# Up projection of a hybrid block: whole PSUM banks are copied by token, and DMAs move the blocks to their features' partitions

## The chip, the cores and the metric

The kernel runs on one core of one Trainium2 chip. The metric is the device time of one execution in microseconds (us). The kernel before takes 1037.89 us, the median of three runs (1037.18 to 1038.49).

## The reference

One layer of a hybrid encoder block in float32, for 256 tokens of width 2048: an input projection, two kinds of attention, an output projection `w_o` with a residual, and then the gated feed-forward part that this case is about:

```python
def conv_gated_ffn(h, w_up, conv_w, conv_b, w_down):
    S = h.shape[1]
    u = h @ w_up
    up = jnp.pad(u, ((0, 0), (CONV_W - 1, 0), (0, 0)))
    c = conv_b + sum(up[:, j:j + S] * conv_w[j] for j in range(CONV_W))
    gate, val = c[..., :D_FF], c[..., D_FF:]
    return (jax.nn.silu(gate) * val) @ w_down
...
        h = rms_norm(x, norm_ffn[l])
        x = x + conv_gated_ffn(h, w_up[l], conv_w[l], conv_b[l], w_down[l])
```

`w_up` is 2048 x 11264 (D_FF is 5632), `w_down` 5632 x 2048. `rms_norm` divides each token by its root mean square and multiplies each feature by a gain. The convolution (width 3) runs over tokens, with taps of each feature's own.

## The kernel before

**Products.** Each float32 operand is split in two: ScalarE copies a weight tile to a rounded type (`hi`, line 641), VectorE subtracts it from the tile (`lo`, line 1000). TensorE makes three products of each pair (hi x hi and lo x hi in `hi2`, lines 1523 and 1524; hi x lo in `lo1`, line 1528). A tile of weights is 512 KB. The stages follow each other: projection in, attention, `w_o`, up projection, down projection, final norm.

**The ring.** Raw tiles lie in a ring of four. SyncE (SP) issues the load of tile t when VectorE has made the `lo` part of tile t - 4 (`load`, lines 427 to 430). ScalarE and VectorE split three tiles ahead of TensorE (`LEAD`): while TensorE works on tile s, they make tile s + 3. ScalarE's split also waits until TensorE is done with tile t - 4, whose split buffer it takes.

**The up stage.** It has 22 steps: 11 pairs `j`, each with `v` = 0 (gate) and `v` = 1 (value). A step is 8 tiles, and gives 256 tokens x 512 features, tokens on partitions, in two PSUM banks: `tr_ps` for `v` = 0, `pj` for `v` = 1. The convolution wants features on partitions. So while TensorE works on the next step, the step just ended is finished by the other engines (its `s` counts the 8 tiles of that next step):

- `s` = 0 to 3: ScalarE copies the 16 blocks of 32 partitions each to other partitions, into `moved` (`move_blocks`, line 857), in groups of 5, 4, 4 and 3. The banks are free for TensorE after the last.
- `s` = 4: VectorE transposes `moved` in 32 x 32 squares into `ub` (line 1257) and multiplies by the tokens' roots, spread over all partitions in `r2b` (`scale_rows`, line 1264). That comes ahead of the `lo` split of tile 7.
- `s` = 5, 6: ScalarE starts the convolution (line 866). `s` = 6, 7: VectorE ends it (lines 1270 and 1274).
- With `v` = 1 also the gate: VectorE's product at `s` = 0 (line 1281), ScalarE's rounded copy (line 878) and VectorE's remainder (line 1286) at `s` = 1.

The order on each engine is the order in which the code is written; semaphores do the rest. TensorE waits for the blocks of two steps ago before it writes a bank again. SP's queue holds only the loads there, and POOL's queue builds sums of `w_down` tiles in DRAM all through the stage. The last step is finished in the first tiles of the down stage, with half of its blocks moved by VectorE (line 1414).

**The roots.** After `w_o`, the tokens' roots are made by VectorE and ScalarE, turned, written to DRAM by four small DMAs (line 844) and read back for all partitions (line 847).

**Other DMAs from SBUF to SBUF.** Attention (line 437) and `w_o` (line 491) already turn blocks with a DMA: four DMAs for each time, each from 32 partitions to all 128.

Of the kernel before, what the change touches and what calls it, by code (L numbers as in the profile page):

```python
# [5 lines left out]
F32 = mybir.dt.float32  # L6
# [5 lines left out]
P = 128  # L12
# [24 lines left out]
UP_DVE_STEPS = 10  # L37
# [88 lines left out]
MOVES = {0: (0, 5), 1: (5, 9), 2: (9, 13), 3: (13, SIDE * SIDE)}  # L126
# [69 lines left out]
def program(nc, x, norm_mix, w_in, sinks, b_f, w_o, norm_ffn, w_up, conv_w, conv_b, w_down, norm_final,  # L196
            ident_c, tri_c, mask_b_c, cos_c, sin_c, out):
    ctx = ExitStack()
    with ctx:
# [6 lines left out]
        def sem(name):  # L206
# [14 lines left out]
        r2b = sb("r2b", [P, S])  # L221
# [7 lines left out]
        region_end = sbuf.cursor  # L229
        sbuf.cursor = region  # L230
# [40 lines left out]
        moved = sb("moved", [P, 4, MT, SIDE, BLOCK])  # L271
# [69 lines left out]
        y_s, yturn_s, yhi_s, ylo_s, ysq_s, y2_tot, y2_root, r2_s, r2_out, d_r2 = (sem(n) for n in (  # L341
            "y_s", "yturn_s", "yhi_s", "ylo_s", "ysq_s", "y2_tot", "y2_root", "r2_s", "r2_out", "d_r2"))
        d_y = [sem(f"d_y{i}") for i in range(2)]
        pad_s, moved_s, moved_d, u_s, c0_s, conv_s, silu_s, gated_s, ghi_s, glo_s = (sem(n) for n in (
            "pad_s", "moved_s", "moved_d", "u_s", "c0_s", "conv_s", "silu_s", "gated_s", "ghi_s", "glo_s"))
# [9 lines left out]
        r2_dram = nc.dram_tensor("r2_dram", (MT, SIDE, BLOCK), F32).ap()  # L355
# [51 lines left out]
        r2_block, r2_rows = conv_o[:, 1, 0, 0:BLOCK], conv_o[:, 0, 0, 0:BLOCK]  # L407
        r2c = r2_block[:, 0:MT]
# [11 lines left out]
        def _(sp):  # L420
# [87 lines left out]
            with sp.Fori(1, UP_PAIRS) as j:  # L508
# [120 lines left out]
        def _(act):  # L629
# [191 lines left out]
            def y_hi_turned(n):  # L821

                act.wait_ge(d_y[n % 2], (n // 2 + 1) * PARTS_Y)
                for b in range(4):
                    k = 4 * n + b
                    act.activation(act_hi[:, k].rearrange("p (a x) -> p a x", a=SIDE), y_turned[n % 2][:, b], ACT.Copy, scale=g2[:, k:k + 1]).then_inc(yhi_s, 1)
# [9 lines left out]
            def root_of_squares(s):  # L836
# [4 lines left out]
                if s == 3:  # L841
                    act.wait_ge(r2_s, 3)
                    for a in range(SIDE):
                        act.dma_start(r2_dram[:, a], r2_rows[a * BLOCK:a * BLOCK + MT]).then_inc(r2_out, 16)
                if s == 5:
                    act.wait_ge(r2_out, 16 * SIDE)
                    act.dma_start(r2b[:], r2_dram.rearrange("m a i -> (m a i)").partition_broadcast(P)).then_inc(d_r2, 16)
# [12 lines left out]
            def conv_first(j, v, pair):  # L860

                act.wait_ge(u_s, step_of(j, v, 2, pair + 1))
# [18 lines left out]
            def finish(j, v, s):  # L881

                if s in MOVES:
                    ins = move_blocks(j, v, *MOVES[s], step_of(j, v, UP_TILES, T_UP + UP_TILES))
                    if MOVES[s][1] == SIDE * SIDE:
                        ins.then_inc(moved_s, 1)
# [51 lines left out]
            half = SIDE * SIDE // 2  # L938
            for t in range(DOWN_END):
                if t == 6:  # L940
# [4 lines left out]
                if t < 2:  # L945
                    ins = move_blocks(*last_step, t * half // 2, (t + 1) * half // 2, T_DOWN)
                if t == 1:
                    ins.then_inc(moved_s, 1)
                if t == 1:
                    silu_gate(UP_PAIRS - 1)  # L950
                if t in (3, 4):
                    conv_first(*last_step, t - 3)
                if t == 7:
# [34 lines left out]
        def _(dve):  # L988
# [230 lines left out]
            def y_lo_turned(n):  # L1219

                for b in range(4):
                    k = 4 * n + b
                    dve.wait_ge(yhi_s, k + 1)
                    dve.scalar_tensor_tensor(act_lo[:, k].rearrange("p (a x) -> p a x", a=SIDE),
                                             y_turned[n % 2][:, b], g2[:, k:k + 1],
                                             act_hi[:, k].rearrange("p (a x) -> p a x", a=SIDE).bitcast(F32),
                                             ALU.mult, ALU.subtract).then_inc(ylo_s, 1)
# [11 lines left out]
            def root_of_squares(s):  # L1239

                if s == 0:
                    dve.memset(r2_block, 0.0).then_inc(r2_s, 1)
                    dve.wait_ge(ysq_s, MT * GROUPS)
                    dve.tensor_reduce(tot2, ss2, AX.X, ALU.add).then_inc(y2_tot, 1)
                if s == 2:
                    dve.wait_ge(y2_root, 1)
                    dve.wait_ge(r2_s, 1)
                    dve.reciprocal(r2c, root2).then_inc(r2_s, 1)
                    dve.wait_ge(r2_s, 2)
                    dve.transpose(r2_rows, r2_block).then_inc(r2_s, 1)  # L1250

            def turn_moved(j, v):

                dve.wait_ge(moved_s, step_of(j, v, 1, 1))
# [669 lines left out]
```

## Time and profile before

| | |
|---|---|
| median of 3 runs | 1037.89 us (1037.18 to 1038.49) |
| span of the profiled execution | 1035.4 us |
| median less span | 2.5 us |
| TensorE busy | 1026.6 us (99%) |
| VectorE busy | 793.9 us (77%) |
| ScalarE busy | 734.5 us (71%) |
| granted TensorE clock, mean | 0.999 |

The span is that of one profiled execution, from its first to its last instruction. No time of its own is given for that execution; the 2.5 us by which the median is above the span is taken for what lies around the span. Busy shares are means over stages. The up stage runs from about 323 us to about 801 us of the span.

### The profile page before, as it was taken

How to read it: one execution, taken by the hardware profiler on the slowest of the kernel's cores; microseconds unless marked ns; L12 is line 12 of the kernel's file. 1: busy time of each engine (PE TensorE's matmuls, PEld its weight loads, DVE VectorE, ACT ScalarE, POOL GpSimd, SP SyncE). 2: the span in 40 equal slices, each digit the busy share in tenths (PEclk: the TensorE clock that was granted, in tenths of full speed). 3: DMA queues.
4: the chain of work that ended last, by engine and by line, in shares of the span. 5: the costliest groups of instructions: out<-in, count | busy, mean ns of one | idle time of the engine just before them, and what ended most of it. 6: DMA issues, size and time to landing. Idle time of an engine off the chain costs nothing.

```text
span 1035.4 us, 15993 instructions
## 1 busy us (share of the span) xinstructions
PE 1026.6 (99%) x5141; PEld 858.3 (83%) x5141; DVE 793.9 (77%) x1026; ACT 734.5 (71%) x1191; POOL 88.9 (9%) x150
## 2 busy tenths in 40 slices
PE   9999999999999999999999999999999999999997
PEld 8888888888888888888888888888888878888885
DVE  5679787887767578768687787876868999887677
ACT  6966474745556687988879888798887766646664
POOL 1000000000111111111111111111111000000000
PEclk9999999999999999999999999999999999999999
DMA  9676767667899999898999998989999589888993
GB/s 295 188 225 178 238 189 224 191 208 215 271 285 321 282 290 269 264 266 278 264 288 254 280 263 269 282 254 278 261 274 264 167 306 316 295 289 285 319 313 113
DMA packets 156103, 266.85 MB, mean 258 GB/s; under 512 B 11908, under 2 KB 60388, under 8 KB 155936
## 3 DMA queue, kind: packets, MB, share of 16 engines
q1 hardware_dynamic: 138224, 222.67, 65.7%
q0 software_dynamic: 17360, 43.22, 18.9%
q8 instruction: 22, 0.36, 0.1%
q10 hardware_dynamic: 480, 0.47, 0.1%
q14 instruction: 17, 0.14, 0.0%
HBM read 256.86 MB, written 44.06 MB: 291 GB/s over the span
## 4 chain that ended last, share of the span: by engine, by line
PE 98%; DMA 1%; SPq 0%; DVE 0%; ACT 0%; issue 0%; DVEq 0%
PE pj L1523 12%; PE pj L1528 12%; PE pj L1524 12%; PE pj L1536 9%; PE tr_ps L1528 9%; PE tr_ps L1523 9%; PE tr_ps L1524 9%; PE pj L1541 5%; PE sc_ps L1528 4%; PE sc_ps L1523 4%; PE sc_ps L1524 4%; PE pj L1558 3%; PE pj L1551 2%; PE pj L1517 1%; PE pj L1519 1%; PE pj L1518 1%
## 5 line engine op out<-in xcount | busy, mean ns | idle before, releaser
L1000 DVE TENSOR_TENSOR split<-raw,split 128x1024 fp32r<-128x1024 f32 x265 | 321.6, 1222 | 159.6 <-ACT split L641 153.8
L641 ACT ACTIVATE split<-raw 128x1024 fp32r<-128x1024 f32 x259 | 272.7, 1056 | 125.1 <-PE pj L1528 26.0
L929 ACT ACTIVATE split<-raw 128x1024 fp32r<-128x1024 f32 (+1 forms) x125 | 121.6, 989 | 63.6 <-PE sc_ps L1528 27.9
L1335 DVE TENSOR_TENSOR split<-raw,split 128x1024 fp32r<-128x1024 f32 (+1 forms) x125 | 138.2, 1136 | 31.0 <-ACT split L929 29.3
L1523 PE MATMUL tr_ps<-split,act_split 128*128 128x512 f32 x352 | 136.9, 389 | 0.0
L1524 PE MATMUL tr_ps<-split,act_split 128*128 128x512 f32 x352 | 136.9, 389 | 0.0
L1523 PE MATMUL pj<-split,act_split 128*128 128x512 f32 x352 | 136.9, 389 | 0.0
L1524 PE MATMUL pj<-split,act_split 128*128 128x512 f32 x352 | 136.9, 389 | 0.0
L1536 PE MATMUL pj<-act_split,split 128*128 128x512 f32 x416 | 131.6, 398 | 0.0
L1528 PE MATMUL tr_ps<-split,act_split 128*128 128x512 f32 x352 | 94.1, 389 | 0.0
L1528 PE MATMUL pj<-split,act_split 128*128 128x512 f32 x352 | 94.1, 389 | 0.0
L1541 PEld LDWEIGHTS pj<-act_split,split 128*128 128x128 f32 x416 | 78.1, 188 | 18.4
L1541 PE MATMUL pj<-act_split,split 128*128 128x256 f32 x416 | 81.8, 278 | 0.0
L1524 PEld LDWEIGHTS pj<-split,act_split 128*128 128x128 f32 x352 | 66.1, 188 | 13.8
L1524 PEld LDWEIGHTS tr_ps<-split,act_split 128*128 128x128 f32 x352 | 66.1, 188 | 13.8
L1528 PEld LDWEIGHTS tr_ps<-split,act_split 128*128 128x128 f32 x352 | 66.1, 188 | 13.7
L1528 PEld LDWEIGHTS pj<-split,act_split 128*128 128x128 f32 x352 | 66.1, 188 | 13.7
L1523 PEld LDWEIGHTS tr_ps<-split,act_split 128*128 128x128 f32 x352 | 66.0, 188 | 13.7
L1523 PEld LDWEIGHTS pj<-split,act_split 128*128 128x128 f32 x352 | 66.0, 188 | 13.7
L857 ACT ACTIVATE moved<-tr_ps 32x256 f32<-32x256 f32 x176 | 66.3, 377 | 2.6
L857 ACT ACTIVATE moved<-pj 32x256 f32<-32x256 f32 x168 | 63.3, 377 | 2.5
L1536 PEld LDWEIGHTS pj<-act_split,split 128*128 128x128 f32 x416 | 63.3, 189 | 1.3 <-issue 1.3
(249 smaller groups left out, 1660.9 us busy)
## 6 DMA issues: line engine op xcount, KB each, us to landing
raw<-w_up SPq DMA_DIRECT2D x176, 512.0 KB, 5.8
raw<-w_in SPq DMA_DIRECT2D x72, 512.0 KB, 4.3
raw<-w_down SPq DMA_DIRECT2D x68, 512.0 KB, 6.0
t_dram<-w_down POOLq DMA_DIRECT2D x60, 512.0 KB, 6.6
raw<-t_dram SPq DMA_DIRECT2D x40, 512.0 KB, 6.0
raw<-w_o SPq DMA_DIRECT2D x32, 512.0 KB, 6.3
t_dram<-t_dram POOLq DMA_DIRECT2D x40, 256.0 KB, 6.6
raw<-w_down SPq DMA_DIRECT2D x20, 256.0 KB, 6.1
```

Source lines behind the costliest of these rows:

```text
L641: ins = act.activation(hi[:, slot, 0:TILE], raw[:, slot, 0:TILE], ACT.Copy)
L857: ins = act.activation(moved[b * BLOCK:(b + 1) * BLOCK, :, a % 2, a // 2::2].rearrange("p w m i -> p m w i"), rows, ACT.Copy)
L929: act.activation(hi[:, slot, c0:TILE], down_raw(t)[:, c0:TILE], ACT.Copy).then_inc(hi_done, 1)
L1000: dve.tensor_tensor(lo[:, slot, 0:n], raw[:, slot, 0:n], hi[:, slot, 0:n].bitcast(F32), ALU.subtract).then_inc(lo_done, 1)
L1335: dve.tensor_tensor(lo[:, slot, c0:TILE], down_raw(t)[:, c0:TILE], hi[:, slot, c0:TILE].bitcast(F32), ALU.subtract).then_inc(lo_done, 1)
L1523: pe.matmul(dst, a_hi, b_hi, start=start, stop=False, skip_group_check=True)
L1524: pe.matmul(dst, a_lo, b_hi, start=False, stop=False, skip_group_check=True)
L1528: return pe.matmul(dst, a_hi, b_lo, start=False, stop=True, skip_group_check=True)
L1536: pe.matmul(pj[:, 2 * pair + b], wh[:, c, b * P:(b + 1) * P], act_both(4 * kt + c), start=first and c == 0, stop=False, skip_group_check=True)
L1541: ins = pe.matmul(pj[:, 2 * pair + b, 0:S], wl[:, c, b * P:(b + 1) * P], act_hi[:, 4 * kt + c], start=False, stop=True, skip_group_check=True)
L1551: pe.matmul(pj[:, 2 + m, 0:S], act_lo[:, 4 * kt + c, m * P:(m + 1) * P], both[:, c, 0], start=first and c == 0, stop=False, skip_group_che ...
L1558: ins = pe.matmul(pj[:, 2 + m], act_hi[:, 4 * kt + c, m * P:(m + 1) * P], both[:, c].rearrange("p a n -> p (a n)"), start=False, stop=True ...
```

## The change

ScalarE copies each of the two banks of a step whole, scaled by the root of the partition's token, into a new tile `token_u`. SP then issues 16 DMAs of 32 KB each from `token_u` to `moved` (`move_u`), which stand in its queue ahead of the load of the third tile of a step (`MOVE_AT`). VectorE waits for all 16, and transposes in two instructions; the product with the roots goes, and so do the roots' way over DRAM, and VectorE's part in moving the last step. TensorE now waits for the evacuation alone. In the down stage the convolution of the last step comes two tiles later. A small rearrangement keeps the tokens of `act_hi` and `act_lo` in another order, for which VectorE's instruction on each block is cut in two.

```diff
-UP_DVE_STEPS = 10
+UP_DVE_STEPS = 8
...
-MOVES = {0: (0, 5), 1: (5, 9), 2: (9, 13), 3: (13, SIDE * SIDE)}
+PARTS_U = 16 * SIDE * SIDE
+MOVE_AT = 2
+LAST_MOVE_AT = 8
...
+            def move_u(j, v):
+
+                sp.wait_ge(evac_u, step_of(j, v, 1, 1))
+                for a in range(SIDE):
+                    for b in range(SIDE):
+                        sp.dma_start(moved[b * BLOCK:(b + 1) * BLOCK, a], token_u[a * BLOCK:(a + 1) * BLOCK, b]).then_inc(d_mv, 16)
+
             def up_loads(j, first):
                 for v in range(2):
                     for kt in range(UP_TILES):
+                        if not first and kt == MOVE_AT:
+                            move_u(j - 1, v)
                         load(step_of(j, v, UP_TILES, T_UP + kt), kt % RING, wide(raw, kt % RING),
...
             for t, (g, kind, part, kt) in enumerate(DOWN):
+                if t in (MOVE_AT, LAST_MOVE_AT):
+                    move_u(UP_PAIRS - 1, (MOVE_AT, LAST_MOVE_AT).index(t))
...
-            def move_blocks(j, v, first, last, tiles_done):
-
-                act.wait_ge(mm_done, tiles_done)
-                if not (isinstance(j, int) and 2 * j + v == 0):
+            def evacuate_u(j, v):
+
+                act.wait_ge(mm_done, step_of(j, v, UP_TILES, T_UP + UP_TILES))
+                if isinstance(j, int) and 2 * j + v == 0:
+                    act.wait_ge(r2_s, 1)
+                else:
                     act.wait_ge(u_s, step_of(j, v, 2, 0))
-                for i in range(first, last):
-                    a, b = divmod(i, SIDE)
-                    rows = up_banks[v][a * BLOCK:(a + 1) * BLOCK].rearrange("p m (w b i) -> p m w b i", w=4, b=SIDE)[:, :, :, b]
-                    ins = act.activation(moved[b * BLOCK:(b + 1) * BLOCK, :, a % 2, a // 2::2].rearrange("p w m i -> p m w i"), rows, ACT.Copy)
-                return ins
+                for m in range(MT):
+                    ins = act.activation(token_u[:, :, m].rearrange("p b w i -> p w b i"),
+                                         up_banks[v][:, m].rearrange("p (w b i) -> p w b i", w=4, b=SIDE), ACT.Copy, scale=r2c[:, m:m + 1])
+                ins.then_inc(evac_u, 1)
...
             def turn_moved(j, v):
 
-                dve.wait_ge(moved_s, step_of(j, v, 1, 1))
+                dve.wait_ge(d_mv, step_of(j, v, PARTS_U, PARTS_U))
                 if not (isinstance(j, int) and 2 * j + v == 0):
                     dve.wait_ge(conv_s, step_of(j, v, 4, 0))
-                st.done(dve.transpose(ub[:, :, 2:S + 2], moved[:].rearrange("p w m a i -> p w (m a i)")))
-
-            def scale_rows():
-
-                st.wait()
-                for pair in range(2):
-                    rows = ub[:, 2 * pair:2 * pair + 2, 2:S + 2]
-                    dve.tensor_tensor(rows, rows, r2b[:].unsqueeze(1).broadcast_to([P, 2, S]), ALU.mult).then_inc(u_s, 1)
+                for m in range(MT):
+                    dve.transpose(ub[:, :, m * P + 2:(m + 1) * P + 2].rearrange("p w (a x) -> p w a x", a=SIDE),
+                                  moved[:, :, m].rearrange("p a w i -> p w a i")).then_inc(u_s, 1)
...
-                    pe.wait_ge(moved_s, step_of(j, v, 1, -1))
+                    pe.wait_ge(evac_u, step_of(j, v, 1, -1))
```

SP's queue in the loop over the pairs, before the change: the loads of a step follow each other, each behind its wait for `lo_done` (the `lo` part of four tiles before).

```order
L430 ISA [waits lo_done]
L430 DMA raw<-w_up 128x2x512
L429 REGISTER_ALU
L430 ISA [waits lo_done]
L430 DMA raw<-w_up 128x2x512
```

The same place after the change, where the loads of a step's second and third tile stood next to each other:

```order
L431 ISA [waits lo_done]
L431 DMA raw<-w_up 128x2x512
L498 REGISTER_ALU
L501 DMA moved<-token_u 32x256 [waits evac_u]
L501 DMA moved<-token_u 32x256 x15
L430 REGISTER_ALU
L431 ISA [waits lo_done]
L431 DMA raw<-w_up 128x2x512
```

Sixteen DMAs now stand between two loads, once in each step.

VectorE at `s` = 4 and 5 of a step with `v` = 0, before the change (`split<-raw` is the `lo` part of tile 7, then of tile 8):

```order
L1256 ISA [waits moved_s]
L1257 STREAM_TRANSPOSE ub<-moved 128x4x256 [waits conv_s]
L177 ISA
L1264 TENSOR_TENSOR ub<-ub,r2b 128x2x256 [waits dve_step]
L1264 TENSOR_TENSOR ub<-ub,r2b 128x2x256
L993 REGISTER_ALU
L1000 TENSOR_TENSOR split<-raw,split 128x1024 [waits hi_done]
```

And after it:

```order
L1259 ISA [waits d_mv]
L1261 STREAM_TRANSPOSE ub<-moved 128x4x128 [waits conv_s]
L1261 STREAM_TRANSPOSE ub<-moved 128x4x128
L997 REGISTER_ALU
L1004 TENSOR_TENSOR split<-raw,split 128x1024 [waits hi_done]
```

The wait ahead of the transposes was one for ScalarE and is now one for the DMAs; the `lo` part of tile 7 stands behind it as before.

## Rows read from the trace of the kernel before

**Rows 1.** The page's first part: busy time, share of the span, instructions.

```profile
PE 1026.6 (99%) x5141; PEld 858.3 (83%) x5141; DVE 793.9 (77%) x1026; ACT 734.5 (71%) x1191; POOL 88.9 (9%) x150
```

**Rows 2.** Windows: busy us by engine (instructions), TensorE clock, DMA share, GB/s.

```profile
320.00:324.00 4.00, 4.00 (x19) 3.30 (x19) 1.54 (x2) 2.04 (x2) 0.52 (x1) 1.00 1.01 365
...
411.00:454.50 43.50, 43.50 (x194) 36.02 (x193) 32.42 (x39) 36.53 (x61) 6.09 (x10) 1.00 0.90 264
454.50:498.00 43.50, 43.50 (x194) 36.02 (x193) 33.88 (x43) 36.64 (x61) 5.84 (x10) 1.00 0.91 277
```

**Rows 3.** Waits of TensorE's weight loads on VectorE: us in total, times, longest.

```profile
PEld pj L1517 <- DVE act_split L1016: 0.8, 1, 0.8
...
PEld sc_ps L1528 <- DVE split L1335: 0.4, 1, 0.4
...
PEld tr_ps L1528 <- DVE split L1335: 0.3, 1, 0.3
```

**Rows 4.** Groups of instructions: busy us, mean ns of one, idle before.

```profile
L857 ACT ACTIVATE moved<-tr_ps 32x256 f32<-32x256 f32 x176 | 66.3, 377 | 2.6
...
L1264 DVE TENSOR_TENSOR ub<-ub,r2b 128x512 f32<-128x512 f32 x44 | 28.5, 688 | 0.8
L1257 DVE STREAM_TRANSPOSE ub<-moved 128x1024 f32<-128x1024 f32 x22 | 27.4, 1246 | 1.2
...
L1216 DVE STREAM_TRANSPOSE prob_t<-nat 128x512 f32<-128x512 f32 x8 | 8.4, 1094 | 0.1
...
L755 ACT ACTIVATE mix_hi<-tr_ps 128x512 f32 x6 | 3.6, 595 | 1.0 <-PE tr_ps L1659 1.0
```

**Rows 5.** Timeline of VectorE around one step: start us, us, instruction.

```profile
454.59 0.88 DVE L1270 SCALAR_TENSOR_TENSOR conv_o<-ub,cst,conv_o 128x256 f32<-128x256 f32 x2
...
456.41 1.23 DVE L1000 TENSOR_TENSOR split<-raw,split 128x1024 fp32r<-128x1024 f32 x1
...
461.81 1.22 DVE L1000 TENSOR_TENSOR split<-raw,split 128x1024 fp32r<-128x1024 f32 x1 [1.28 <-ACT split L641]
...
468.12 1.22 DVE L1000 TENSOR_TENSOR split<-raw,split 128x1024 fp32r<-128x1024 f32 x1
...
477.98 1.23 DVE L1281 TENSOR_TENSOR conv_o<-conv_o 128x1024 f32<-128x1024 f32 x1
479.12 2.36 DVE L1000 TENSOR_TENSOR split<-raw,split 128x1024 fp32r<-128x1024 f32 x2
```

**Rows 6.** Timeline of TensorE: first product of that step, last four of its tile 7.

```profile
453.78 0.39 PE L1523 MATMUL tr_ps<-split,act_split 128*128 128x512 f32 x1
...
474.63 1.07 PE L1528 MATMUL tr_ps<-split,act_split 128*128 128x512 f32 x4
```

**Rows 7.** Timeline of SP: the load issued behind the `lo` part of tile 5.

```profile
463.20 0.37 SPq L430 DMA_DIRECT2D raw<-w_up  x1
```

**Rows 8.** Line 430, loads of `w_up`: ns to issue (min/median/max), us to landing.

```profile
L430 SPq DMA_DIRECT2D raw<-w_up x176: 362/373/592, 310.6 to 785.1; - x176
...
DMA to landing us min/median/max: 3.4/5.5/11.4
```

**Rows 9.** Line 491, SBUF to SBUF, 32 partitions to 128: ns to issue, us to landing.

```profile
L491 SPq DMA_DIRECT2D prob<-prob_t x16: 548/604/654, 275.2 to 330.2; - x16
...
DMA to landing us min/median/max: 2.8/3.2/8.0
```

**Rows 10.** Line 537, results from 128 partitions, behind each other: issue, landing.

```profile
L537 SPq DMA_DIRECT2D result<-nat x9: 333/442/453, 1025.7 to 1031.6; - x9
...
DMA to landing us min/median/max: 1.9/2.4/3.4
```

**Rows 11.** Line 844, ScalarE's queue, 2 partitions each: ns to issue.

```profile
L844 ACTq DMA_DIRECT2D r_dram<-conv_o x4: 242/275/482, 331.7 to 332.7; - x4
```

**Rows 12.** Line 437, SBUF to SBUF in the attention stage: ns to issue.

```profile
L437 SPq DMA_DIRECT2D prob<-prob_t x48: 542/603/1054, 91.0 to 249.7; - x48
```

More of the change, by code:

```diff
@@ L229, in program @@
         region_end = sbuf.cursor
+        sbuf.cursor = region_end - 4 * 4 * S
+        token_u = sb("token_u", [P, SIDE, MT, 4, BLOCK])
         sbuf.cursor = region
@@ L406, in program @@
         root2 = small[:, 38:40]
-        r2_block, r2_rows = conv_o[:, 1, 0, 0:BLOCK], conv_o[:, 0, 0, 0:BLOCK]
-        r2c = r2_block[:, 0:MT]
+        r2c = small[:, 40:42]
         g1 = cst[:, 0:KB]
@@ L507, in _ @@
             up_loads(0, True)
-            with sp.Fori(1, UP_PAIRS) as j:
+            up_loads(1, False)
+            with sp.Fori(2, UP_PAIRS) as j:
                 up_loads(j, False)
             for t, (g, kind, part, kt) in enumerate(DOWN):
+                if t in (MOVE_AT, LAST_MOVE_AT):
+                    move_u(UP_PAIRS - 1, (MOVE_AT, LAST_MOVE_AT).index(t))
                 if t < RING:
@@ L881, in finish @@
             def finish(j, v, s):
[L883 to L886, printed above, removed]
+                if s == 0:
+                    evacuate_u(j, v)
                 if s in (5, 6):
@@ L937, in _ @@
             last_step = (UP_PAIRS - 1, 1)
-            half = SIDE * SIDE // 2
             for t in range(DOWN_END):
-                if t == 6:
+                if t == 8:
                     act.activation(small[:, 24:25], eps, ACT.Sqrt)
@@ L944, in _ @@
                     down_hi(t + LEAD)
[L945 to L948, printed above, removed]
+                if t == 0:
+                    evacuate_u(*last_step)
                 if t == 1:
                     silu_gate(UP_PAIRS - 1)
-                if t in (3, 4):
-                    conv_first(*last_step, t - 3)
-                if t == 7:
+                if t in (5, 6):
+                    conv_first(*last_step, t - 5)
+                if t == 9:
                     gated_hi(UP_PAIRS - 1)
@@ L1246, in root_of_squares @@
                     dve.wait_ge(y2_root, 1)
-                    dve.wait_ge(r2_s, 1)
                     dve.reciprocal(r2c, root2).then_inc(r2_s, 1)
-                    dve.wait_ge(r2_s, 2)
-                    dve.transpose(r2_rows, r2_block).then_inc(r2_s, 1)
             def turn_moved(j, v):
-                dve.wait_ge(moved_s, step_of(j, v, 1, 1))
+                dve.wait_ge(d_mv, step_of(j, v, PARTS_U, PARTS_U))
                 if not (isinstance(j, int) and 2 * j + v == 0):
                     dve.wait_ge(conv_s, step_of(j, v, 4, 0))
-                st.done(dve.transpose(ub[:, :, 2:S + 2], moved[:].rearrange("p w m a i -> p w (m a i)")))
-            def scale_rows():
-                st.wait()
-                for pair in range(2):
-                    rows = ub[:, 2 * pair:2 * pair + 2, 2:S + 2]
-                    dve.tensor_tensor(rows, rows, r2b[:].unsqueeze(1).broadcast_to([P, 2, S]), ALU.mult).then_inc(u_s, 1)
+                for m in range(MT):
+                    dve.transpose(ub[:, :, m * P + 2:(m + 1) * P + 2].rearrange("p w (a x) -> p w a x", a=SIDE),
+                                  moved[:, :, m].rearrange("p a w i -> p w a i")).then_inc(u_s, 1)
             def conv_rest(j, v, pair):
@@ L1304, in up_step @@
                             turn_moved(p, b)
-                            if first:
-                                dve.wait_ge(d_r2, 16)
-                            scale_rows()
                         if s == 0 and v == 1 and not first:
@@ L1407, in gain @@
                                          gfin[:, n * 512:(n + 1) * 512], ALU.mult)
-            def move_blocks(first, last):
-                for i in range(first, last):
-                    a, b = divmod(i, SIDE)
-                    rows = up_banks[1][a * BLOCK:(a + 1) * BLOCK].rearrange("p m (w b i) -> p m w b i", w=4, b=SIDE)[:, :, :, b]
-                    dve.tensor_copy(moved[b * BLOCK:(b + 1) * BLOCK, :, a % 2, a // 2::2].rearrange("p w m i -> p m w i"), rows).then_inc(moved_d, 1)
-            half = SIDE * SIDE // 2
-            dve.wait_ge(mm_done, T_DOWN)
             for t in range(DOWN_END):
-                if t == 2:
-                    dve.wait_ge(moved_d, half)
-                if t == 2:
+                if t == 4:
                     turn_moved(UP_PAIRS - 1, 1)
@@ L1428, in _ @@
                     down_lo(t + LEAD)
-                if t < 2:
-                    move_blocks(half + t * half // 2, half + (t + 1) * half // 2)
-                if t == 2:
-                    scale_rows()
-                if t in (4, 5):
-                    conv_rest(UP_PAIRS - 1, 1, t - 4)
-                if t == 6:
+                if t in (6, 7):
+                    conv_rest(UP_PAIRS - 1, 1, t - 6)
+                if t == 8:
                     gate(UP_PAIRS - 1)
-                if t == 7:
+                if t == 9:
                     gated_lo(UP_PAIRS - 1)
```

41 lines of the change are left out of this document (18 added, 23 removed).

## The prediction

> **What bounds the kernel now.** I read the page's first part, then windows of two whole steps each in the up stage, then the waits of TensorE, then the timelines of VectorE, TensorE and SP through one step. The page has TensorE busy for 1026.6 us of 1035.4 [rows 1], and in the windows it is busy for all of 43.50 us, with the full clock, while VectorE has 9.6 to 11.1 us free and ScalarE 6.9 [rows 2]. The waits on VectorE add up to 1.5 us, and none is in the up stage [rows 3]. So TensorE's own work is the bound: two steps are 43.5 us, a step 21.75, a tile 2.72. Work taken off ScalarE or VectorE there buys nothing; the question is what the new chain of waits costs.
>
> **What goes.** ScalarE: 16 copies of 0.377 us in a step, 6.0 us, become 2 of about 0.60 (a copy of 128x512 from PSUM, 595 ns) [rows 4], 1.2 us. VectorE: two products of 0.688 go. The transpose of 1.246 us becomes two of half the width: between 0.62 each (half of it) and 1.09 (line 1216, as wide, but it picks every fourth element) [rows 4]. I take 0.62, because the new one reads whole runs of 32 as the old one does; the other end would cost 0.95 us more in a step. All of this is hidden under TensorE. The end of the block moves by VectorE, the roots' way over DRAM, and the cut of VectorE's 16 instructions at the `w_o` stage come to a few us on engines that TensorE doesn't wait for there: 0, bounds -1.5 (all of the waits in [rows 3]) and +1. In the down stage the convolution starts two tiles later, with five tiles left until its result is wanted: 0.
>
> **What comes: a chain round SP, the DMAs and VectorE.** In SP's queue the 16 DMAs stand behind the load that waits for the `lo` part of tile 5. They must all land before VectorE transposes, and behind the transpose stands the `lo` part of tile 7, which TensorE wants at 474.63, that is 20.85 us after the step's start at 453.78 [rows 6]. How long are they?
>
> - Start. VectorE made the `lo` part of tile 5 from 461.81, and the load went out at 463.20 [rows 5, 7], 9.4 us after the start. ScalarE's block copies hold that back now; without them the rounded copy of tile 5 starts when TensorE starts tile 2, at 5.45, and ends at about 6.5, the `lo` part at 7.8, and the load's issue (0.37, [rows 8]) at 8.3.
> - Issue. No DMA of before goes from 32 partitions to 32. The nearest rows: 0.604 us for one from 32 partitions to 128, SBUF to SBUF [rows 9], and 0.603 for others of that kind [rows 12]; 0.442 for results behind each other from 128 partitions [rows 10]; 0.373 for a load [rows 8]; 0.275 for one of two partitions [rows 11]. With a gap of 0.03 from one to the next the pitch is between 0.30 and 0.64. The new DMA moves 32 plain rows on both sides, which puts it between the one of 2 rows and those of 128, and it has no change of shape between its sides, which the 0.604 has. I take 0.40. Fifteen pitches are 6.0 us (4.5 to 9.6).
> - Landing of the last, from the start of its issue: 2.4 median in rows 10, 3.2 in rows 9 of which 0.6 is issue. I take 2.6 (2.3 to 3.2).
>
> First step: 8.3 + 6.0 + 2.6 = 16.9, transposes 1.25, `lo` part 1.22 (the length in [rows 5]): 19.4. TensorE wants it at 20.85, so it has 1.45 us to spare.
>
> But the chain closes on itself. The next 16 DMAs wait for the `lo` part of the next step's tile 5, and VectorE works in order: from one pair of transposes to that point it has 7 `lo` parts. Two successive steps, added up:
>
> - VectorE: 4 transposes 2.5; 14 `lo` parts at 1.2 (2.36 for two behind each other, 1.22 alone, [rows 5]) 16.8; 16 convolution instructions, four of which take 454.59 to 456.41, 1.85 with their gaps [rows 5], 7.4; gate product and its remainder at 1.15 each (477.98 to 479.12, [rows 5]) 2.3. Sum 29.0.
> - SP and DMAs, twice: 0.1 for the hand-over, 0.4 for the load, 6.0, 2.6: 9.1 each, 18.2.
>
> Together 47.2 us against TensorE's 43.5: 3.7 in two steps, 1.85 in one. That VectorE is free for a quarter of the time [rows 2] doesn't help, as it sits in front of the wait. ScalarE isn't in the chain: the load of the third tile goes out 6.4 us after the DMAs' start, lands 5.5 later [rows 8], at 11.9, and VectorE wants its `lo` part at about 15.5.
>
> There are 21 turns of a step inside the up stage, 20 distances between them. TensorE is late at the end by 20 x 1.85 - 1.45 = 35.5 us, and can't win it back, since it has no idle time to give. Span 1035.4 + 35.5 = 1070.9; with the 2.5 us by which the median of the runs is above the span, 1073.4.
>
> The Trainium skill speaks against this size. Its page "DMA: Bandwidth & Descriptors", in the section on the anatomy of one DMA, puts most of a DMA's fixed 2 us down to the wait for the write's receipt and calls the making of descriptors small; "SBUF — State Buffer", on the set-up-cost knee, gives sequencer and descriptor work as some 50 ns and a few hundred. With 0.25 us as an estimate from that page the chain would fit and the change would cost nothing, which is the first rival below. The trace has no SBUF-to-SBUF issue under 0.54 [rows 9, 12]; it sides against the low end.
>
> **The rivals.**
>
> 1. *The chain fits, and the time stays.* It decides at one number: 2 x (0.5 + 15 x pitch + landing) + 29.0 = 43.5, so pitch x 15 + landing = 6.75, a pitch of 0.29 with a landing of 2.4. For it: an issue of 0.275 on a small DMA [rows 11]. Against: the other rows are all above 0.33. VectorE wouldn't hold TensorE up, and the time would be 1038. Chance 0.15.
> 2. *The issue costs what rows 9 and 12 have.* Pitch 0.64: 15 x 0.64 + 2.6 = 12.2, two steps 29.0 + 25.4 = 54.4, 5.45 too much in each; the first turn is late by 2.15 at once. 20 x 5.45 + 2.15 = 111, time 1149. For it: the same kind of memory on both sides, the same 32 source partitions, runs of 1 KB. Against: there 128 rows stand on the target side. Chance 0.17.
> 3. *The DMA engines become the bound.* A step moves about 270 GB/s x 21.75 us = 5.9 MB at a share of 0.905 [rows 2]; full share at that mix is 298 GB/s. 0.52 MB more makes 6.4 MB, 21.5 us: it just fits. If the moves take twice their share it is 23.2, and 20 steps cost 29 us: 1067. Against: a stretch of 4 us ran at 365 GB/s [rows 2]. Chance 0.08.
> 4. *Faster.* The engines that feed TensorE have more room, and the waits of rows 3 and the tail shrink: 1.5 us at most, 1036.4. A gain past 0.2% would need more than all of them. Chance 0.03.
>
> **How the numbers follow.** The forecast, the chain with a pitch of 0.33 to 0.50, has 0.57; its own range is 1045 (pitch 0.33 with a landing of 2.4: 15.7 + 29.0 = 44.7, 0.6 in a step) to 1110 (pitch 0.50 with 2.8: 3.45 in a step, and 0.25 late at the first turn, 69; 1107). The range for 8 in 10 takes in the upper bound of the issue, 1149, and at the low end reaches just over rival 1, whose time is the floor of the likely ones: 1038 to 1150. Within 0.2% is 1035.8 to 1040.0, about what a measurement of this kernel can tell from no change. Faster 0.03; the same 0.15; slower 0.57 + 0.17 + 0.08 = 0.82.
>
> **What would show it.** In the profile after: TensorE has idle time in the up stage, in front of the third product (line 1528 of before), released by VectorE's `lo` part, once in each step at tile 7, and about 3.7 us in two steps. VectorE's largest new wait is that of the transposes for the DMAs from `token_u`. SP issues the 16 in about 6.4 us. ScalarE is busy for about 27 us of two steps where it had 36.6. The down stage keeps its length. I am wrong if TensorE stays at its 43.5 us for two steps (the issue is cheap), if it waits for rounded copies that wait for raw tiles (the loads are the bound, rival 3), or if the waits stand in the down stage.

## The result, and the profile after

The changed kernel takes 1169.61 us (median of 4 runs, 1165.20 to 1171.50) against 1037.72 for the kernel before: a ratio of 1.126 (95% interval 1.124 to 1.129), 131.9 us slower. Ratios here and below are of fast executions alone; one slow execution of the kernel before, of 3689 us beside the first experiments, is not in them. The forecast was 1073 with a range up to 1150. The sign and the place were right, the size was not: the loss is 3.7 times the one forecast, and above rival 2's too.

The page of the kernel after, busy time by engine and the granted clock in 40 slices:

```profile
PE 1064.5 (91%) x5141; PEld 878.6 (75%) x5141; DVE 760.1 (65%) x1010; ACT 634.0 (54%) x891; POOL 89.9 (8%) x150
...
PEclk9999999999999989898988989999989999999999
...
PE 47%; SPq 18%; DVE 15%; DMA 10%; issue 7%; ACT 2%; DVEq 1%; ACTq 0%
```

Against [rows 1] VectorE has lost 34 us of work and ScalarE 100, as the change meant, and the span has grown from 1035.4 to 1165.9. The third line, the shares of the chain that ended last, has 18% of SP issuing and 10% of DMAs landing. TensorE's busy time has risen by 38 us with the same 5141 products; the clock line shows where: the slices below full clock are all in the up stage. The run `fill` below prices that.

Window of the kernel after, the stretch of [rows 2] in one piece (busy us by engine, clock, DMA share, GB/s):

```profile
411.00:498.00 87.00, 72.85 (x299) 58.93 (x298) 44.10 (x56) 43.60 (x51) 9.55 (x16) 0.92 0.82 226
```

TensorE was busy for all 87 us and is now for 72.85, with 299 products recorded where there were 388. The share of the DMA engines was 0.90 to 0.91 and is 0.82: they are not what is short. The waits say what is:

```profile
DVE ub L1261 <- DMA moved<-token_u: 239.7, 22, 13.3
ACT conv_o L875 <- DVE ub L1261: 168.1, 21, 11.6
...
ACT split L654 <- DMA raw<-w_up: 75.1, 50, 5.0
...
PE pj L1510 <- DVE split L1004: 55.0, 11, 8.3
...
PE tr_ps L1510 <- DVE split L1004: 33.4, 10, 5.4
```

VectorE waits 22 times for the moves, 10.9 us each on average; TensorE waits 21 times for VectorE's `lo` part, once in a step. (In [rows 3] the waits on VectorE were under 1 us each.) The timeline of SP shows the reason in its length: 10.0 us for 16 moves, with the loads queued behind them.

```profile
500.88 13.36 SPq L431 DMA_DIRECT2D raw<-w_up  x7
514.40 10.03 SPq L501 DMA_DIRECT2D moved<-token_u  x16
524.68 17.54 SPq L431 DMA_DIRECT2D raw<-w_up  x8
542.32 10.09 SPq L501 DMA_DIRECT2D moved<-token_u  x16
552.77 0.38 SPq L431 DMA_DIRECT2D raw<-w_up  x1
```

The chain of waits in 515 to 569 us (start, us, what) is the closed ring, piece by piece: moves, their landing, VectorE's transposes, its `lo` parts, a load, and the next moves. It has no TensorE in it; between its lines below stand more of the moves and VectorE's `lo` parts and convolution instructions:

```profile
514.97 0.59 SPq L501
515.60 0.59 SPq L501
...
523.20 0.59 SPq L501
523.84 4.80 DMA moved<-token_u
...
529.30 0.67 DVE ub L1261
529.97 2.24 DVE split L1004 x2
...
539.27 2.42 DVE split L1004 x2
541.84 0.37 SPq L431
542.32 0.51 SPq L501
...
551.20 0.58 SPq L501
551.82 2.17 DMA moved<-token_u
```

From 514.97 to 515.60 is the pitch: 0.63 us. Over most of the up stage (345 to 920 us) the chain isn't as pure: issues of moves are 32.5% of it and their landing 10.4%, but raw tiles' landing is 5.0% and TensorE's products at least 9.3%. All moves of the kernel (ns to issue, min/median/max; us to landing):

```profile
L501 SPq DMA_DIRECT2D moved<-token_u x352: 512/591/1175, 353.4 to 941.3; - x176
...
DMA to landing us min/median/max: 1.8/3.5/7.2
```

**Where the 130.5 us of span went.** TensorE's first product of the up stage starts at 323.12 (323.22 before), its first of the down stage at 924.24 (801.94 before): 122.4 us in the up stage. Another 8.2 us are in the down stage (233.5 us before, 241.7 after). There the last step's moves still hold VectorE up, and TensorE then waits for it 1.0 us at 947.6 and 2.6 us at 960.5; the clock is below its full value in parts of the stage (0.85 in 924 to 934 us, 0.86 in 954 to 964). The two waits are 3.5 us, and TensorE is busy for 230.5 us of the stage where it was for 226.6: 7.4 of the 8.2 us. With four DMAs in place of 16 on the same queue (`four`), or with nobody waiting for four (`cut4`), the down stage has 233.4 and 233.5 us. VectorE's timeline there, and TensorE's wait at the first turn (window 323 to 370):

```profile
943.24 1.30 DVE L1261 STREAM_TRANSPOSE ub<-moved 128x512 f32<-128x512 f32 x2 [6.64 <-DMA moved<-token_u]
...
PE pj L1510 <- DVE split L1004: 1.3, 1, 1.3
```

In the up stage the 20 distances between the transposes (364.74 to 920.46 us) average 27.79 us where a step was 21.75: 20 x 6.04 = 120.8. The rest, 1.6, is mostly the first turn, where TensorE waited for the 1.3 us in the line above.

Worked out over those 20 distances from the timelines of SP and VectorE, with the same for three kernels of the experiments:

| mean, us | turn to first move | SP issuing | end of issue to turn | step | 20 x (step - 21.75) | measured loss |
|---|---|---|---|---|---|---|
| forecast | 15.0 | 6.4 | 2.2 | 23.6 | 37 | |
| after, 16 moves | 15.19 | 10.12 | 2.48 | 27.79 | 121 | 131.9 |
| `eight` | 15.29 | 5.23 | 4.80 | 25.32 | 71 | 71.6 |
| `four` | 15.47 | 2.64 | 6.08 | 24.19 | 49 | 50.1 |
| `r4sp` | 15.16 | 2.82 | 7.40 | 25.38 | 73 | 77.7 |

The last two columns agree because the loss lies in the up stage, evenly over its steps; of what `r4sp` and the kernel after lose beyond that, most is in the down stage. What makes a step long is in the three columns before.

### The profile page after: what moved, and what is told of

The parts are those of the page before. It is cut to its first block, busy times and chain, and to the rows that moved or that the text cites. A ratio compares the mean times of both kernels' runs of the same rounds, so it can differ in the third digit from the quotient of the medians.

```text
span 1165.9 us, 15889 instructions
## 1 busy us (share of the span) xinstructions
PE 1064.5 (91%) x5141; PEld 878.6 (75%) x5141; DVE 760.1 (65%) x1010; ACT 634.0 (54%) x891; POOL 89.9 (8%) x150
## 4 chain that ended last, share of the span: by engine, by line
PE 47%; SPq 18%; DVE 15%; DMA 10%; issue 7%; ACT 2%; DVEq 1%; ACTq 0%
SPq L501 17%; DVE split L1004 9%; PE pj L1518 8%; DMA moved<-token_u 5%; PE pj L1510 5%; PE pj L1523 4%; DMA raw<-w_up 4%; PE pj L1505 4%; PE pj L1506 4%; PE sc_ps L1510 3%; PE sc_ps L1505 3%; PE sc_ps L1506 3%; PE pj L1540 3%; PE tr_ps L1505 2%; PE tr_ps L1506 2%
## 5 line engine op out<-in xcount | busy, mean ns | idle before, releaser
L1004 DVE TENSOR_TENSOR split<-raw,split 128x1024 fp32r<-128x1024 f32 x265 | 317.9, 1217 | 93.5 <-ACT split L654 87.3
L654 ACT ACTIVATE split<-raw 128x1024 fp32r<-128x1024 f32 x259 | 273.0, 1058 | 193.2 <-DMA raw<-w_up 75.1
L1261 DVE STREAM_TRANSPOSE ub<-moved 128x512 f32<-128x512 f32 x44 | 28.7, 690 | 239.7 <-DMA moved<-token_u 239.7
L1510 PE MATMUL pj<-split,act_split 128*128 128x512 f32 x352 | 102.5, 416 | 55.0 <-DVE split L1004 55.0
L1505 PE MATMUL tr_ps<-split,act_split 128*128 128x512 f32 x352 | 143.6, 408 | 0.0
L1506 PE MATMUL tr_ps<-split,act_split 128*128 128x512 f32 x352 | 142.5, 405 | 0.0
L1505 PE MATMUL pj<-split,act_split 128*128 128x512 f32 x352 | 141.3, 402 | 0.0
L1506 PE MATMUL pj<-split,act_split 128*128 128x512 f32 x352 | 141.2, 401 | 0.0
L875 ACT ACTIVATE conv_o<-ub,cst 128x256 f32<-128x256 f32 x88 | 47.8, 590 | 168.1 <-DVE ub L1261 168.1
L1510 PE MATMUL tr_ps<-split,act_split 128*128 128x512 f32 x352 | 99.0, 404 | 33.4 <-DVE split L1004 33.4
L1510 PEld LDWEIGHTS pj<-split,act_split 128*128 128x128 f32 x352 | 69.5, 201 | 74.0 <-DVE split L1004 59.7
L1510 PEld LDWEIGHTS tr_ps<-split,act_split 128*128 128x128 f32 x352 | 67.4, 194 | 51.5 <-DVE split L1004 37.7
L1505 PEld LDWEIGHTS tr_ps<-split,act_split 128*128 128x128 f32 x352 | 70.2, 199 | 15.4
L1506 PEld LDWEIGHTS tr_ps<-split,act_split 128*128 128x128 f32 x352 | 70.1, 199 | 15.4
L1505 PEld LDWEIGHTS pj<-split,act_split 128*128 128x128 f32 x352 | 68.9, 196 | 14.9
L1506 PEld LDWEIGHTS pj<-split,act_split 128*128 128x128 f32 x352 | 68.7, 195 | 14.9
```

The costliest lines, as they stand in the source:

```text
L654: ins = act.activation(hi[:, slot, 0:TILE], raw[:, slot, 0:TILE], ACT.Copy)
L875: act.activation(conv_o[:, v, w], ub[:, w, 2:S + 2], ACT.Identity, scale=tap(2, j * 4 + (w + v * FB)), bias=tap(3, j * 4 + (w + v * FB))). ...
L1004: dve.tensor_tensor(lo[:, slot, 0:n], raw[:, slot, 0:n], hi[:, slot, 0:n].bitcast(F32), ALU.subtract).then_inc(lo_done, 1)
L1505: pe.matmul(dst, a_hi, b_hi, start=start, stop=False, skip_group_check=True)
L1506: pe.matmul(dst, a_lo, b_hi, start=False, stop=False, skip_group_check=True)
L1510: return pe.matmul(dst, a_hi, b_lo, start=False, stop=True, skip_group_check=True)
```

## The experiments

Each time is a median; beside it stands the kernel before, run on the same chip (1037.4 to 1038.6 us).

**micro: what an issue costs, by itself.** A small program, executed once, in which SP issues DMAs in groups of 8 or 4 with nothing else running. (At its end ScalarE issues eight while SP writes the results; these had a median of 0.765 us, outside of what theory A expected, and with SP busy beside them they don't tell what ScalarE's queue costs by itself.)

```
sp.dma_start(cross[b*32:(b+1)*32, a], src[a*32:(a+1)*32, b])   # 32 rows of 1 KB; short: 128 B; pair: 16 rows
sp.dma_start(full[:, ...], src[:, ...])                        # 128 rows of 512 B; fan: 32 partitions to 128
sp.dma_start(d32[...], src[...])                               # to DRAM; down, wide: from DRAM
sp.dma_start(alone[...], src[...]); wait                       # one at a time
```

> This kernel computes nothing of the block: it only issues small DMAs of several forms in groups, and writes zeros. It measures the issue by itself. Theory A (the issue of a DMA from SBUF to SBUF costs about 0.59 us whatever its size, because of the kind): 32 rows of 1 KB, 32 rows of 128 B, 16 rows and 128 rows from SBUF to SBUF all take 0.55 to 0.65 us to issue, on SP as on ScalarE's queue, and those with DRAM on one side 0.33 to 0.45. Theory B (the cost comes from the rows or from a full queue of descriptors): 16 rows or 128 B rows issue in under 0.45 us, the 128 rows take over 0.8, and a DMA that is issued alone takes under 0.45.

```profile
L51 SPq DMA_DIRECT2D cross<-src x8: 565/590/596, 3.0 to 7.5; - x8
L57 SPq DMA_DIRECT2D short<-src x8: 507/591/592, 9.3 to 13.6; - x8
L62 SPq DMA_DIRECT2D full<-src x8: 528/601/602, 15.3 to 19.8; - x8
L67 SPq DMA_DIRECT2D fan<-src x4: 605/611/629, 21.7 to 23.7; - x4
L73 SPq DMA_DIRECT2D d<-src x8: 362/422/423, 26.3 to 29.5; - x8
L79 SPq DMA_DIRECT2D down<-w_down x8: 355/421/423, 31.1 to 34.3; - x8
L84 SPq DMA_DIRECT2D wide<-w_down x4: 349/432/432, 36.0 to 37.3; - x4
L90 SPq DMA_DIRECT2D pair<-src x8: 581/589/591, 39.9 to 44.3; - x8
L96 SPq DMA_DIRECT2D alone<-src x8: 507/507/507, 46.1 to 58.5; - x8
```

The medians fall into two values: 0.59 to 0.61 us where both sides are SBUF, 0.42 to 0.43 where one is DRAM (`d` and `down` have the 32 rows of 1 KB of `cross`). Rows (16, 32, 128) and row length (128 B to 1 KB) change it by 0.02 at most. Issued singly it is 0.507, the value of the first one in a step of the kernel. Landing with the engines idle has medians of 1.7 to 1.9 us from SBUF to SBUF, 2.6 for `fan`.

**four: a quarter of the DMAs, the same bytes, the wait kept.** The 32x32 blocks are not exchanged, so what VectorE turns is not the reference's.

```
                 for a in range(SIDE):
-                    for b in range(SIDE):
-                        sp.dma_start(moved[b * BLOCK:(b + 1) * BLOCK, a], token_u[a * BLOCK:(a + 1) * BLOCK, b]).then_inc(d_mv, 16)
+                    sp.dma_start(moved[:, a], token_u[:, a]).then_inc(d_mv, 16)
```

> The changed kernel with the 512 KB of a step moved by 4 DMAs of 128 rows of 1 KB, partition to same partition, in place of 16 of 32 rows: same bytes, same waits, blocks not moved to their features' partitions. Theory A (a closed chain of SP's issues, the landing, and VectorE's order): a step of 27.8 us loses 12 issues of 0.63, 7.6 us, and is 20.2, under TensorE's 21.75; time 1038 to 1043, TensorE's waits in the up stage under 3 us in all. Theory B (the bytes on the DMA engines are the bound): nothing or little changes, 1150 or more. Theory C (each DMA costs by its rows): 128 rows take four times the issue, and the time stays at 1150 or more as well, but with SP's issues at 2.4 us.

1088.73 us, ratio 1.050 (1.045 to 1.054): 81 us less than the kernel after, but 50 above before, where none was expected. The issue did shrink to 2.64 us; the landing grew.

```profile
L500 SPq DMA_DIRECT2D moved<-token_u x88: 470/601/2176, 353.2 to 858.0; - x88
...
DMA to landing us min/median/max: 3.4/5.9/10.4
```

5.9 us to land, not 1.9 as in `full` (of half the size). In the kernel after a long issue hid this. Worked out from the trace, the first of its 16 moves lands 5.2 us after the start of its issue on average and the last 3.0, where the four of `four` have 5.8 to 6.7. `short` below, with an eighth of the bytes, has the same 5.0 falling to 2.9, so it isn't the moves' own bytes. The likely reason is that no load is added while SP issues the 16, and the last finds the engines free; that is argued, not shown. Issue time taken away comes back in part as landing: of 7.48 us less, 3.60.

**cut: the 16 DMAs stay, VectorE doesn't wait for them.** VectorE turns `token_u` itself, unexchanged. ScalarE's next copies wait for the moves, since these read `token_u`; no such wait shows in the trace.

```
-                dve.wait_ge(d_mv, step_of(j, v, PARTS_U, PARTS_U))
+                dve.wait_ge(evac_u, step_of(j, v, 1, 1))
```

> The changed kernel, but VectorE transposes token_u itself, as soon as ScalarE has written it; the 16 DMAs are issued in the same place and nobody but ScalarE's next evacuation (and the first use of their memory in the down stage) waits for them. Blocks aren't moved. It keeps SP's blocked queue, the late loads and the traffic, and takes the wait away. Theory A (chain through VectorE's wait): 1038 to 1045; SP's 10.1 us of issues in a step of 21.75 fit beside 8 loads of 0.4. Theory B (SP's queue holds back the loads of raw tiles, and TensorE starves for them): TensorE still waits, for rounded copies that wait for raw tiles, and the time is above 1080.

1113.15 us, ratio 1.072 (1.068 to 1.076). The wait is gone and 75 us of loss are there all the same. The two views of `cut`, waits and SP's timeline:

```profile
ACT split L654 <- DMA raw<-w_up: 222.5, 93, 9.6
...
577.47 10.03 SPq L501 DMA_DIRECT2D moved<-token_u  x16
587.86 14.27 SPq L431 DMA_DIRECT2D raw<-w_up  x8
602.28 3.06 SPq L501 DMA_DIRECT2D moved<-token_u  x5
```

From moves to moves it is 24.8 us: 10.0 in which no load goes out, and 14.3 in which all eight of a step have to (the row takes in SP's waits for free tiles). The held queue makes the loads late, and ScalarE waits for raw tiles. The prediction had taken the loads to be safe (the load of the third tile "goes out 6.4 us after the DMAs' start" and lands "at 11.9, and VectorE wants its `lo` part at about 15.5"); with 10 us of issue they are not.

**early: the moves at the step's start** (`MOVE_AT` 2 becomes 0), everything computed.

> The changed kernel with the 16 DMAs two loads earlier in SP's queue (MOVE_AT 0). Theory A: between the transposes and the next DMAs VectorE has 5 lo parts in place of 7, 2.4 us less in a step, and the remainder of the gate product (1.15 in two steps) falls behind them: a step is 27.8 - 2.4 - 0.6 = 24.8, time 1169.6 - 20 x 3.0 = 1110 (1100 to 1120). Theory B (DMA engines or SP as a whole are the bound): no change, 1165 to 1172.

1151.15 us (1146.25 and 1156.05), ratio 1.108 (1.102 to 1.115): 18 us less than the kernel after, not the 50 to 70 expected. Its waits:

```profile
ACT split L654 <- DMA raw<-w_up: 255.3, 77, 11.6
DVE ub L1261 <- DMA moved<-token_u: 182.1, 22, 11.1
```

The wait for raw tiles was 75.1 us in the kernel after. From a turn to the first move it is 14.4 us where it was 15.2: 0.8 us less, not 3.0, because VectorE's `lo` parts in between now wait for late raw tiles. Their landing is 15.9% of the chain over the stage, in the kernel after 5.0%. The cost of `cut` comes in place of what the earlier moves gain.

**cut4: four DMAs, VectorE doesn't wait.** `cut` with the DMAs of `four`.

> As the kernel in which VectorE transposes token_u itself (nobody waits for the DMAs), with 4 DMAs of 128 rows for the 16: SP is held for 2.5 us in a step where it was held for 10.1, and the same 512 KB go over the DMA engines. Blocks aren't moved to other partitions. Two causes are on the table. Theory A' (two separate costs: SP's held queue, and VectorE's wait for the landing): with both gone the time is 1037 to 1042. Theory B' (0.5 MB more in a step on DMA engines that are already busy for 0.9 of it costs by itself): 1050 to 1090, with ScalarE waiting for raw tiles.

1037.53 us (10 runs) against 1037.40, ratio 1.000 (0.999 to 1.001). Its window:

```profile
411.00:498.00 87.00, 87.00 (x385) 72.05 (x384) 61.42 (x77) 55.14 (x65) 11.89 (x20) 1.00 0.95 295
```

The same bytes are moved, at a DMA share of 0.95, and TensorE is busy for all 87.00 us. So 0.5 MB more in a step costs nothing (rival 3), and neither does anything else the change did to ScalarE and VectorE.

**r4act and r4sp: the whole computation with four DMAs.** Token 4i+a is put on the place of token 32a+i, so that each DMA takes all 128 partitions to 32; the roots are put in that order by two small DMAs ahead of the stage. `r4act` issues them on ScalarE right behind its copies, `r4sp` on SP at `MOVE_AT` 2.

```
+   act_hi[:, k].rearrange("p (m i a) -> p a m i", m=MT, a=SIDE)      # and act_lo likewise
+   for b in range(SIDE):
+       act.dma_start(moved[b*BLOCK:(b+1)*BLOCK], token_u[:, b])       # r4sp: sp.dma_start
```

> The changed kernel with correct blocks in 4 DMAs from 128 partitions to 32, issued by ScalarE behind its evacuation: the tokens stand interleaved on the partitions (a column order of act_hi and act_lo), and the roots are put in the same order by two small DMAs. VectorE waits for them as in the changed kernel. In the kernel with 4 DMAs on SP's queue the last landed 5 to 10 us after it was issued, against 1.9 to 2.6 for such DMAs by themselves. Theory A' (on SP's queue they stand in the same rings behind up to 4 raw tiles of 512 KB): on ScalarE's own queue they land within 3.5 us, long before s = 4, and the time is 1037 to 1042. Theory B' (the DMA engines are busy, whichever queue): the landing stays at 5 to 8 us. They are issued about 2.6 us after the step's start and may take 8, so the transposes at 10.9 would hardly wait either, but TensorE still loses time to late raw tiles: over 1050.

1038.12 us (10 runs) against 1037.40, ratio 1.001 (1.000 to 1.002): the time of the kernel before. The moves, and ScalarE's and VectorE's timelines in one step of `r4act`:

```profile
L869 ACTq DMA_DIRECT2D moved<-token_u x88: 554/626/1503, 350.9 to 807.8; - x88
...
DMA to landing us min/median/max: 2.8/5.4/11.4
...
459.80 2.61 ACTq L869 DMA_DIRECT2D moved<-token_u  x4
...
467.85 1.31 DVE L1263 STREAM_TRANSPOSE ub<-moved 128x512 f32<-128x512 f32 x2 [0.64 <-DMA moved<-token_u]
```

The expectation had a quick landing on a queue of its own; that part fell: 5.4 us, as slow as on SP. The time is kept by an early start, by SP's queue left to the loads, or by both; the two stay together here. The step begins at 455.22 for TensorE; the moves start 4.6 us into it (3.5 on average, in the kernel after 11.1), as soon as ScalarE has its copies and without any work of VectorE before them, and the turn is at 12.6, with VectorE waiting 0.64 us. In the kernel before, the place behind tile 5's `lo` part is 9.4 us into the step [rows 5 to 7]. The 8 us from the first issue to the turn are there, but in no ring.

> The same as the kernel with 4 DMAs on ScalarE's queue, but issued by SP ahead of the third load, as in the changed kernel. Both theories: as the kernel with 4 DMAs of 128 rows partition to same partition, 1080 to 1095. If the shape of the DMAs (128 rows to 32) mattered more than the queue, it would be outside of this.

1115.13 us, ratio 1.075 (1.072 to 1.077), above the 1080 to 1095 expected. A step is 1.19 us longer than in `four`, 24 us in 20 steps, and the landing is the cause: 7.40 us for 6.08 from the end of the issue to the turn. The down stage is longer too, 240.9 us for 233.4 (profiled executions). Its moves:

```profile
L502 SPq DMA_DIRECT2D moved<-token_u x88: 559/618/1395, 353.9 to 883.7; - x88
...
DMA to landing us min/median/max: 4.8/6.5/12.1
```

Why 128 partitions to 32 land later than 128 to 128 is open.

**short: 16 DMAs with an eighth of the bytes.** Rows of 128 B instead of 1 KB; the rest of `moved` is zero.

> The changed kernel with its 16 DMAs on SP cut to 128 B in each of the 32 rows, 64 KB in a step for 512; the rest of moved stays zero. Theory A' (the issue, 0.59 whatever the size, and the order in the rings): 1150 to 1172, issues of 0.59 and a landing under 2.5 us behind the last issue. Theory B' (bytes): it falls by more than half of the loss, under 1105.

1169.97 us, ratio 1.128 (1.125 to 1.130), the time of the kernel after. The bytes of the moves don't count, their number does.

**r4early: `r4sp` with `MOVE_AT` 0.**

> Correct blocks in 4 DMAs from 128 partitions to 32, issued by SP, two loads earlier in its queue (MOVE_AT 0). It was 1115 at the old place, and 1038 on ScalarE's queue, where they also go out some 4 to 5 us earlier. Theory P (the place decides: the landing of 6.5 us is the same on both queues, and it only has to start by about 5 us into the step, with SP held 2.6 us and not 10): from the transposes to the next DMAs VectorE has 5 lo parts, so a step's chain is 1.3 + 6.0 + 3.7 + 0.6 + 0.5 + 1.9 + 6.5 = 20.5 us, under 21.75: 1037 to 1045. Theory Q (the queue decides: on SP's queue any such DMA holds back raw tiles and lands behind them): over 1070.

1056.14 us (1051.19 to 1061.87), ratio 1.019 (1.015 to 1.023), between the two expectations. Its waits:

```profile
ACT split L655 <- DMA raw<-w_up: 163.5, 85, 6.9
...
DVE ub L1269 <- DMA moved<-token_u: 99.0, 22, 9.7
```

Of `r4sp`'s 78 us above the kernel before, the place accounts for 60. With the 18 us left ScalarE waits 163.5 us for raw tiles, in `r4act` 68.2. But the start isn't the same either: the moves go out 8.4 us into TensorE's step on average, in `r4act` 3.5, because on SP they stand behind a load that waits for VectorE. So what remains may come from the queue or from the later start; no run parts the two.

**fill: does the lower clock cost anything?** 16 products more in 20 of the 22 steps, into a bank that is free, in front of TensorE's wait.

> The changed kernel with 16 matmuls of 128x512 more on TensorE in each step (into a PSUM bank that the up stage doesn't use), between the second product of a step's tile 7 and the wait for VectorE's lo part: they fill 3.6 us of the 4.2 that TensorE waits there, and keep its clock. Theory A' (TensorE isn't in the chain, the lower granted clock of 0.963 costs nothing): 1163 to 1175, clock above 0.98. Theory C (part of the 132 us is the slower clock, up to the 38 us by which TensorE's busy time grew): 1130 to 1150.

1166.31 us, ratio 1.123 (1.121 to 1.125), with a mean clock of 0.982 in place of 0.963. TensorE's busy time rises to 1120.7 us and the time hardly moves (3 us less; the intervals of the two ratios overlap). The 38 us that TensorE's products take longer in the kernel after stand where it would have waited: the ring sets the pace.

**eight: between 4 and 16.** Eight DMAs of 64 rows, the halves exchanged instead of the blocks.

> The changed kernel with the 512 KB in 8 DMAs of 64 rows, with the blocks' halves exchanged (not the right partitions). SP is held 5.0 us; in the kernels with 4 and with 16 the last has landed 8.5 and 12.5 us after the first one's issue. Theory A': max of about 8.5 (the engines' backlog) and 5.0 + 2 to 4, so 8.5 to 9: between the 1089 of 4 DMAs and the 1170 of 16, but near the lower: 1090 to 1115. If the loss went by the count alone it would be 1089 + 81 x 4/12 = 1116 or more.

1109.97 us, ratio 1.069 (1.067 to 1.071). Issue 5.23, end of issue to turn 4.80: both terms lie between those of `four` and of the kernel after. The time is in the range expected, its working is not: the last move is used 10.0 us after the first one's issue, not 8.5 to 9.

## Why the prediction was wrong in its size

- **What bounds the kernel before: right.** `cut4` and `r4act` relieve ScalarE and VectorE as the change does (ScalarE is busy for 55 and 56 us of 87 where [rows 2] have 73) and gain nothing.
- **What goes: right,** though on no path. The median copy of 128x512 by ScalarE took 0.676 us (0.60 forecast), a half transpose 0.691 (0.62, upper bound 1.09).
- **The ring: right.** It is the chain of waits above, and TensorE waits once in a step in front of its third product, as foretold. The first moves went out 8.5 us into their step (8.3 forecast), and VectorE's part with SP's load was forecast at 15.0 us a step and is 15.2.
- **The step that failed is the issue: "I take 0.40".** It is 0.59, with a pitch of 0.63. Fifteen pitches are 9.5 us, not 6.0: 3.5 us a step, 71 us in 20. The choice went by the number of rows and the plainness of the shape, which `micro` shows to count for 0.02 us; what counts there is whether DRAM is on one side. Rows that said so stood there: [rows 9, 12] are SBUF to SBUF and have 0.60; [rows 8, 10, 11] have DRAM on one side and 0.37, 0.44 and 0.28 (the last, of two partitions on ScalarE's queue, was not tried again). They were used as ends of a range, and the value was taken between two kinds, of which only one applies. Here the issue is 0.59 of the 3.07 us from the start of the last issue to the turn, and sixteen in series are 10.1 us of a step of 27.8. The Trainium skill's page "DMA: Bandwidth & Descriptors" (anatomy of one DMA) calls the making of descriptors small, but that section describes DMAs issued from GpSimd, and the moves are issued from SP.
- **The landing was short by half a microsecond.** 3.07 us from the last issue's start (2.48 + 0.59) where 2.6 was taken: 0.47 a step, 9 us. Its range (to 3.2) held it; the chain's 4.80 us piece shows that single ones do not keep to it.
- **The first turn** was to have 1.45 us to spare and came some 1.4 late (TensorE's wait there was 1.3 us): 2.9 us (the pitch alone would make it 3.5; this once the landing was shorter, the turn following 1.9 us after the last issue's start).
- **The down stage** was to keep its length, a term put at nothing ("with five tiles left until its result is wanted: 0"), and took 8.2 us more: the last step's moves are as long on their way as the others, VectorE stands still for 6.64 us, and TensorE waits for it and runs at a lower clock for a while.
- **The ends of the range** have small slips: with a pitch of 0.33 its working gives 1047 and not 1045, with 0.50 a step is 3.55 too long and not 3.45, 1109.
- The sum: 70.6 + 9.4 + 3.8 (VectorE's 0.19 a step) + 2.9 + 8.2 = 94.9 of the 95.0 us between the forecast span's growth (35.5) and the measured one (130.5). It must nearly close, as nearly the whole up stage is steps and first turn.
- **Rival 2,** the issue of rows 9 and 12, came nearest (1149). It had the pitch, and lacks the landing, VectorE's 0.19 and the down stage.
- **Rival 3** is excluded by `short` and `cut4`, **rival 1** by the pitch, **rival 4** by the sign.
- **What the prediction had not seen:** a second cost. The same 10 us hold the loads behind them, 75 us by itself (`cut`). Neither in `cut4`, 0; the wait with four DMAs in `four`, 50; the held loads without the wait in `cut`, 75; both in the kernel after, 132. That 50 and 75 nearly give 132 doesn't make them its two parts: `four` has a longer landing and late raw tiles too (15.8% of its chain), while in the kernel after the chain is nearly all ring, with raw tiles' landing in 5.0% of it for 28.6% in `cut`. How far the two costs add is not shown. "ScalarE isn't in the chain" is nearly true of the kernel after, false as soon as the moves start early.

The version that the experiments point to, `r4act`, is as fast as the kernel before and not faster; TensorE's work is the bound of both (busy for 87.00 us of 87 in either).

## What to carry to other kernels

Price the issue of a DMA by the kind of memory on its two sides, from a row of the same kind, and multiply by the count: many small DMAs in one queue are paid in issue time, and whatever stands behind them (here the loads) is held up by it as well. When a wait is added on an in-order engine, look whether what it waits for is itself started by work behind the previous wait: what the ring is longer than the bound's step is lost in each step, and what stands at its end, here the down stage, is to be priced too. If such moves are needed, use few, start them as soon as the data is there, and put them on a queue that holds no loads; here the last two came together in `r4act`, and how much each gives is not shown.

## What the runs showed of the hardware

- Issue on SP's queue, behind each other: 0.59 to 0.61 us from SBUF to SBUF, alike for 16 to 128 rows and for rows of 128 B and 1 KB, and 0.42 to 0.43 with DRAM on one side (32 and 128 rows). Issued singly 0.51 from SBUF to SBUF; the loads of the up stage, between waits, have 0.37. On ScalarE's queue the moves of `r4act` had 0.63.
- Landing of moves of 128 KB in the up stage: 5.9 us on SP (`four`, 128 partitions to 128), and from 128 to 32 6.5 on SP (`r4sp`) and 5.4 on ScalarE's queue (`r4act`), against 1.9 for 64 KB with nothing else running. A queue of their own doesn't bring it back.
- From 128 partitions to 32 the last of the four moves was there 1.3 us later than from 128 to 128 (`r4sp` and `four`); not explained.
- TensorE's clock, windows of the kernel after around one of its waits:

```profile
524.00:528.00 4.00, 0.00 (x0) 0.00 (x0) 0.00 (x0) 0.00 (x0) 0.00 (x0) 0.96 1.01 219
528.00:532.00 4.00, 0.88 (x2) 0.78 (x3) 3.34 (x4) 1.85 (x3) 0.00 (x0) 0.50 0.17 64
532.00:536.00 4.00, 4.00 (x14) 3.15 (x14) 3.83 (x7) 3.97 (x6) 0.00 (x0) 0.69 0.90 290
536.00:540.00 4.00, 4.00 (x19) 3.34 (x18) 3.85 (x7) 3.24 (x5) 1.05 (x1) 1.00 0.79 235
```

After a wait of 8.3 us the clock is at its lower level (0.50, 1.2 GHz), products take 0.63 instead of 0.39 us, and it is back at 2.4 GHz (1.00) in the last window. With 16 products in the wait (`fill`) the mean clock was 0.982 in place of 0.963, and the time stayed within the noise.
